# State-space parameters, tables and sines moved from the state-space stage into the first attention and feed-forward stages

## The chip, the cores and the metric

The kernel runs on one NeuronCore of a Trainium2 chip. The core has five engines with a queue of their own each: TensorE (PE, matrix multiplications, with PEld for its weight loads), VectorE (DVE), ScalarE (ACT), GpSimd (POOL) and SyncE (SP), which here only issues DMAs. They meet at semaphores. The metric is the device time of one launch in microseconds (us), the median of several runs. Everything is float32; the large products are computed from two-part splits (a high part and the remainder) in three matrix multiplications.

## What is computed

Two blocks of two layers each over a sequence of 512 tokens of 1024 channels. The kernel runs them as eight stages: two attention layers, then feed-forward, state-space (S5) mixer, feed-forward, feed-forward, convolution mixer, feed-forward. The part that the change touches is the S5 mixer:

```python
def s5_mixer(h, w_in, a_re, a_im, log_dt, b_re, b_im, c_re, c_im, d_skip, w_glu, b_glu, w_out):
    u = (h @ w_in).reshape(bsz, seq, 64, 16)
    dt = jnp.exp(log_dt)[:, None]
    mag = jnp.exp(dt * a_re)
    abar_re, abar_im = mag * jnp.cos(dt * a_im), mag * jnp.sin(dt * a_im)
    den = ar * ar + ai * ai
    nr = abar_re - 1.0
    f_re, f_im = (nr * ar + abar_im * ai) / den, (abar_im * ar - nr * ai) / den
    bb_re, bb_im = ...            # f * b, complex
    st = associative_scan(abar, bb @ u)           # over the 512 tokens
    y = Re(c @ st) + d_skip * u
    y = jax.nn.gelu(y)
    return (y * jax.nn.sigmoid(y @ w_glu + b_glu)) @ w_out
```

Nothing in `abar`, `f`, `bb` or in the powers and angles of `abar` depends on the tokens.

## The kernel before

The activation X stays in SBUF, channels on partitions, as 8 tiles of 128 x 512. Each stage has a function for each engine (`ffn_pe`, `ffn_act`, `s5_dve`, ...), and the order on an engine is the order in which these functions are written: nothing reorders it. Weights are streamed: SP loads a block of 128 x 2048 into one of two slots (`raw`), ACT copies its high part (`split_h`, L326), DVE takes the remainder (`split_l`, L331), and PE multiplies (`mm3`, L345 to L347, in `pe_block256`); a slot is used again when PE is through with it. In a feed-forward stage a pass of the loop (`pair`) is four tiles on PE: two of W1 and two of W3. ACT does two silus, a split, two copies of the hidden tile (L725) and a second split.

The S5 stage is cut into 8 chunks of tokens of length 8 within 64 positions (CL = 8, NC = 64) and worked off in 8 groups of channels, k = 0 to 7. Its course:

1. `in_pair` and two more blocks give u; `u_tile(o)` on DVE scales tile o, copies it in turned order into `rms`, and SP writes it to device memory with 8 DMAs. `u_tile(o)` waits with its copies until the DMAs of tile o-1 have landed.
2. DVE copies C (L1979), then computes the parameters on 128 x 64 tiles (L1982 to L2007 and L2028 to L2058), the phases of the powers 0 to 8 (L2014 to L2023, on 128 x 576), their products with the magnitudes (L2041 to L2046) and the scaled input matrices B1 and B2 (L2063 to L2073, on 128 x 1024). ACT gives exp and sines for it. `matrices(0)` (L2087 to L2090, six instructions) follows.
3. The loop over k. PE: `to_rows(k+1)` (8 transposes L1758, 8 products L1765), a swap of z (L1799), `toeplitz(k+1)` (L1775), `inputs(k+1)` (L1787), and the outputs of k (L1811, L1812). DVE: the turned inputs and the scan, which gives z(k) (L2113 to L2119), after the swap x(k) (L2127 to L2130), then `phases(k+2)` (L1910 to L1926, ten instructions) and `matrices(k+2)`. ACT: `rows(k+1)`, the sines `waves(k+2)`, the copy YS of the output (L1879), and `kernel_copy(k+1)` (L1863), for which `to_rows(k+2)` waits on PE since both use the same two banks. POOL: `decay(k)` (L2185) and `outmat(k)` (L2175 to L2178), which starts when the outputs of k-1 are through and for which the outputs of k wait. POOL also computes `phases(0)` and `phases(1)`.
4. SP carries YS through device memory to YR. After the loop DVE adds the skip (L2140), ACT applies gelu and takes the high part (L1885, L1888) for the 8 tiles one after another, DVE takes the remainders (L2144), and only behind all that do the splits of the next two weight blocks stand (L326, L331).

In the first attention stage `ahead` on ACT and `tiles` on DVE run in a loop while PE multiplies; in the feed-forward stages POOL has no work between `squares_pool` and the first squares of the output.

## Time and profile before

| what | us |
|---|---|
| median of 3 runs | 3165.71 (3160.33 to 3166.04) |
| the profiled execution's own time | 3160.42 |
| its span in the trace | 3158.6 |
| PE busy | 2817.4 (89%) |
| DVE busy | 1726.3 (55%) |
| ACT busy | 1149.2 (36%) |
| POOL busy | 354.2 (11%) |
| the S5 stage, 1297 to 1745 us: PE busy | 313.08 of 448 |
| the first feed-forward's loop, 943 to 1190 us: PE busy | 247.00 of 247 |

Times in the trace count from the span's start. The granted clock (PEclk) is given as a share of TensorE's full speed: 1.00 is 2.4 GHz, 0.50 is 1.2 GHz. A group has line, engine, operation, tiles, shapes, count, then busy us and mean ns, then idle us before it and what ended it. A timeline row has start, duration, engine, line, operation, the tiles written and read with their shapes, how many instructions are merged, and in brackets how long the engine stood idle before and what ended it. Busy PE time is modelled from pipelined multiplications; POOL's spans are rough.

### The profile page before, as it was taken

To read this page: it belongs to the slowest core of one execution; us is meant where nothing else is said; L and a number is where in the kernel's file an instruction comes from. 1 tells how busy PE (TensorE), PEld (TensorE's weight loads), DVE (VectorE), ACT (ScalarE), POOL (GpSimd) and SP (SyncE) were. 2 spreads that over 40 slices of the span, in tenths; PEclk is the share of its full clock that TensorE was granted. 3 is DMA by queue.
4 is the path that set the end of the run, shared out by engine and by line. 5 is a ranking of instruction groups with operands and counts; after the bars stand their busy time and mean duration, and the time that the engine had idled before them with its cause. 6 is when DMAs were issued, how large, how long until landed. Compare 5 with 4: busy or idle time off the path is not lost.

```text
span 3158.6 us, 37190 instructions
## 1 busy us (share of the span) xinstructions
PE 2817.4 (89%) x13972; PEld 2315.5 (73%) x13972; DVE 1726.3 (55%) x2526; ACT 1149.2 (36%) x1932; POOL 354.2 (11%) x307
## 2 busy tenths in 40 slices
PE   6987978979799999927768999999999998699998
PEld 5855767746588888827757888888888886588887
DVE  4378755388754442577744544254442588554423
ACT  3237833157733222302233322233222366432222
POOL 1011011020020000144311000020000112210000
PEclk9987989967999999966779999999999999899999
DMA  3220012310013323411122222322223211122232
GB/s 125 95 79 1 1 41 91 98 40 1 1 54 96 100 80 92 111 48 28 38 67 69 91 93 85 92 90 93 93 81 100 86 53 41 41 80 94 88 92 73
DMA packets 289664, 222.77 MB, mean 71 GB/s; under 512 B 43379, under 2 KB 285628, under 8 KB 289276
## 3 DMA queue, kind: packets, MB, share of 16 engines
q1 hardware_dynamic: 288604, 216.56, 22.8%
q0 software_dynamic: 928, 4.46, 0.4%
q8 instruction: 82, 1.34, 0.2%
q14 instruction: 50, 0.41, 0.0%
HBM read 214.70 MB, written 6.29 MB: 70 GB/s over the span
## 4 chain that ended last, share of the span: by engine, by line
PE 74%; DVE 10%; issue 5%; ACT 4%; DVEq 3%; POOLq 3%; POOL 2%; SPq 1%; DMA 0%; ACTq 0%
PE bank L345 22%; PE bank L347 21%; PE bank L346 21%; DVE WL L331 2%; PE bank L1316 1%; ACT WH L326 1%; PE bank L1303 1%; PE bank L1328 1%; DVE stats L1600 1%; POOLq L2179 1%; DVE XL L403 1%; DVE CV L984 1%; POOLq L2177 1%; PE bank L1330 1%; PE bank L1329 1%
## 5 line engine op out<-in xcount | busy, mean ns | idle before, releaser
L345 PE MATMUL bank<-XH,WH 128*128 128x512 f32 (+1 forms) x2688 | 999.2, 372 | 83.9 <-DVE WL L331 29.1
L347 PE MATMUL bank<-XH,WL 128*128 128x512 f32 (+1 forms) x2688 | 987.5, 367 | 0.0
L346 PE MATMUL bank<-XL,WH 128*128 128x512 f32 (+1 forms) x2688 | 983.2, 366 | 0.0
L331 DVE TENSOR_TENSOR WL<-raw,WH 128x2048 fp32r<-128x2048 f32 (+1 forms) x212 | 443.2, 2091 | 559.4 <-ACT WH L326 559.0
L345 PEld LDWEIGHTS bank<-XH,WH 128*128 128x128 f32 x2688 | 516.4, 192 | 178.2 <-DVE WL L331 40.4
L326 ACT ACTIVATE WH<-raw 128x2048 fp32r<-128x2048 f32 (+1 forms) x212 | 370.1, 1746 | 592.3 <-PE bank L347 592.3
L346 PEld LDWEIGHTS bank<-XL,WH 128*128 128x128 f32 x2688 | 516.8, 192 | 90.0 <-issue 1.0
L347 PEld LDWEIGHTS bank<-XH,WL 128*128 128x128 f32 x2688 | 515.6, 192 | 90.1
L345 PE MATMUL bank<-HH,WH 128*128 128x512 f32 (+1 forms) x792 | 294.0, 371 | 0.0
L347 PE MATMUL bank<-HH,WL 128*128 128x512 f32 (+1 forms) x792 | 293.7, 371 | 0.0
L346 PE MATMUL bank<-HL,WH 128*128 128x512 f32 (+1 forms) x792 | 291.7, 368 | 0.0
L725 ACT ACTIVATE HH<-work 128x512 f32 (+1 forms) x88 | 55.7, 633 | 369.6 <-DVE work L790 369.6
L834 POOL TENSOR_TENSOR ssq<-ssq,sq 128x512 f32<-128x512 f32 x24 | 30.9, 1290 | 1353.2 <-ACT sq L747 1353.2
L346 PEld LDWEIGHTS bank<-HL,WH 128*128 128x128 f32 x792 | 148.8, 188 | 29.1
L347 PEld LDWEIGHTS bank<-HH,WL 128*128 128x128 f32 x792 | 148.9, 188 | 28.4
L345 PEld LDWEIGHTS bank<-HH,WH 128*128 128x128 f32 x792 | 148.7, 188 | 27.1
L721 ACT ACTIVATE work<-work 128x512 f32<-128x512 f32 x88 | 55.2, 632 | 280.9 <-DVE work L783 280.8
L788 DVE TENSOR_TENSOR work<-bank,rstd 128x512 f32<-128x512 f32 x88 | 60.8, 691 | 175.9 <-PE bank L347 172.1
L783 DVE TENSOR_TENSOR work<-bank,rstd 128x512 f32<-128x512 f32 x88 | 60.2, 688 | 167.4 <-PE bank L347 158.0
L1451 ACT ACTIVATE E<-bank,stats 128x512 f32<-128x512 f32 (+1 forms) x176 | 113.0, 645 | 48.0 <-DVE stats L1602 31.0
L1600 DVE TENSOR_REDUCE stats<-bank 128x1 f32<-128x512 f32 (+1 forms) x176 | 107.8, 634 | 27.2 <-PE bank L1305 26.0
L414 POOL TENSOR_TENSOR ssq<-ssq,sq 128x256 f32<-128x256 f32 x112 | 96.3, 860 | 118.5 <-ACT sq L394 112.9
(364 smaller groups left out, 3599.4 us busy)
## 6 DMA issues: line engine op xcount, KB each, us to landing
raw<-in_ffn_w_dram SPq DMA_DIRECT2D x88, 1024.0 KB, 5.3
raw<-in_ffn_w_dram SPq DMA_DIRECT2D x64, 704.0 KB, 4.6
raw<-in_w_in_dram SPq DMA_DIRECT2D x24, 1024.0 KB, 5.2
raw<-in_w_out_dram SPq DMA_DIRECT2D x8, 1024.0 KB, 5.1
raw<-in_cv_w_in_dram SPq DMA_DIRECT2D x8, 1024.0 KB, 5.5
raw<-in_w_mem_kv_dram SPq DMA_DIRECT2D x4, 1024.0 KB, 5.3
raw<-in_s_w_in_dram SPq DMA_DIRECT2D x4, 1024.0 KB, 6.3
raw<-in_s_w_glu_dram SPq DMA_DIRECT2D x4, 1024.0 KB, 5.4
```

What stands on the lines that cost most here:

```text
L326: act.activation(WH[:, slot, 0:n * P], raw[:, slot, 0:n * P], ACT.Copy).then_inc(h_done, 1)
L331: dve.tensor_tensor(WL[:, slot, 0:n * P], raw[:, slot, 0:n * P], WH[:, slot, 0:n * P].bitcast(F32), ALU.subtract).then_inc(l_done, 1)
L345: pe.matmul(out, WH[:, slot, c:c + P], h, start=start, stop=False)
L346: pe.matmul(out, WH[:, slot, c:c + P], l, start=False, stop=False)
L347: return pe.matmul(out, WL[:, slot, c:c + P], h, start=False, stop=stop)
L414: ins = pool.tensor_tensor(ssq[:, HALF[h]], ssq[:, HALF[h]], sq[:, k % 2, HALF[h]], ALU.add)
L721: act.activation(work2[:, o, :], work1[:, o, :], ACT.Silu).then_inc(ss(s, "silu"), 1)
L725: act.activation(HH[:, bass.ds(2 * i + o, 1), :], work1[:, o, :], ACT.Copy).then_inc(ss(s, "hh"), 1)
L783: dve.tensor_tensor(work1[:, o, :], bank[o][:, :], rstd[:, :], ALU.mult).then_inc(acc_read, 1)
L788: dve.tensor_tensor(work1[:, o, :], bank[2 + o][:, :], rstd[:, :], ALU.mult).then_inc(acc_read, 1)
L1451: act.activation(E[:, m % 6, 0:nk * P], bank[m % 4][:, 0:nk * P], ACT.Exp, bias=stats[:, 1, m % 8:m % 8 + 1], scale=scale, accum_out=stats ...
L1600: dve.tensor_reduce(stats[:, 0, c:c + 1], bank[(m + i) % 4][:, 0:nk * P], AX, ALU.max)
```

## The change

- **First attention stage** (`attn0`). SP loads the S5 parameters behind its first four weight blocks (`par_sp`, five small DMAs). PE turns them after the memory blocks (`par_pe`, three small products). ACT takes exp, exp and two sines between the splits of the weight blocks; DVE computes the 128 x 64 part in three pieces behind three `tiles`. The loops of ACT and DVE there are written out. The results (FH, FL, MAG, FR, FI) stay in a new tile `par`.
- **First feed-forward stage** (`ffn0`). SP loads constants and B behind its first pair of blocks (`tab_sp`). POOL computes the table of powers and B1, B2 (`tab_pool`), sends them to device memory, and then wraps the phases for all 8 groups. ACT computes the sines (`tab_act`, `waves_act`) between the splits, at written places in its now unrolled loop, and issues their DMAs to device memory. The cosine is now taken as a sine of pi/2 less the absolute value, so that a group of phases needs 7 POOL instructions and not 10.
- **S5 stage.** Parameters, tables and phases are gone from DVE, ACT and POOL; SP loads the tables back, ACT issues the loads of the sines (`cs_load`). The skip, gelu and its splits are done inside the loop, for group k-2 and k-3 in pass k.
- MAG to the eighth power is read from `PW`.

```diff
         def ffn_sp(sp, s):
             pair(0)
+            if tab_stage(s):
+                tab_sp(sp, s)
             with sp.Fori(1, NP) as i:
...
+        def tab_sp(sp, s):
+            sp.wait_ge(mm_done, first_step[s])
+            sp.dma_start(s5cA[:, :], io["s5_c"]).then_inc(ss(s, "tab_c"), 16)
...
+            for dst, src in ((B1A[0:64], br), (B1A[64:128], bi), (B2A[0:64], bi), (B2A[64:128], br)):
+                sp.dma_start(dst, src).then_inc(ss(s, "b_in"), 16)
...
+        def wrap(pool, x, n, fh, fl, jj):
+            pool.tensor_tensor(x, fh, jj, ALU.mult)
+            pool.drain()
+            pool.tensor_scalar(n, x, ROUND, -ROUND, ALU.add, ALU.add)
+            pool.drain()
+            pool.tensor_tensor(x, x, n, ALU.subtract)
+            pool.drain()
+            pool.tensor_tensor(n, fl, jj, ALU.mult)
+            pool.drain()
+            pool.tensor_tensor(x, x, n, ALU.add)
+            pool.drain()
+            pool.tensor_scalar(n, x, ROUND, -ROUND, ALU.add, ALU.add)
...
+            pool.dma_start(tab_scr, tabA[:, :]).then_inc(ss(s, "tab_out"), 16)
+            for k in range(KD):
...
+                wrap(pool, PHA[:, :, :], PHN[:, :, :], fh, fl, jc)
+                if k >= 2:
+                    pool.wait_ge(ss(s, f"cs_out{k % 2}"), 16 * (k // 2))
+                pool.tensor_tensor(CSA[:, k % 2, 1], PHA[:, :, :], PHN[:, :, :], ALU.subtract).then_inc(ss(s, "ph"), 1)
...
+        def waves_act(act, s, k):
+            act.wait_ge(ss(s, "ph"), at(s, "ph", k + 1))
+            cos, sin = CSA[:, k % 2, 0], CSA[:, k % 2, 1]
+            act.activation(cos, sin, ACT.Abs).then_inc(ss(s, "abs"), 1)
+            act.wait_ge(ss(s, "abs"), at(s, "abs", k + 1))
+            act.activation(sin, sin, ACT.Sin, scale=s5cA[:, S5_SGN + 2:S5_SGN + 3])
+            act.activation(cos, cos, ACT.Sin, bias=eps_c[:, 1:2], scale=-TURN).then_inc(ss(s, "waves"), 1)
+            act.wait_ge(ss(s, "waves"), at(s, "waves", k + 1))
+            act.dma_start(cs_scr[k], CSA[:, k % 2]).then_inc(ss(s, f"cs_out{k % 2}"), 16)
...
         def ffn_act(act, s):
...
+            def pair(i, nxt, middle=()):
...
+                for k in middle:
+                    waves_act(act, s, k)
                 hidden(i, 0)
                 hidden(i, 1)
                 split_h(act, b0 + 2 * i + 3, 1, nxt, s0 + 4 * i + 4)
...
+            if tab_stage(s):
+                pair(1, 16)
+                tab_act(act, s)
+                pair(2, 16)
+                pair(3, 16)
+                waves_act(act, s, 0)
+                pair(4, 16, (1,))
+                waves_act(act, s, 2)
+                act.wait_ge(ss(s, "tab_out"), at(s, "tab_out", 16))
+                pair(5, 16, (3,))
+                waves_act(act, s, 4)
+                pair(6, 16, (5,))
+                waves_act(act, s, 6)
+                pair(7, 16, (7,))
+                for k in range(2):
+                    act.wait_ge(ss(s, f"cs_out{k}"), 16 * (KD // 2))
+                pair(8, 16)
+                pair(9, 16)
...
         def s5_sp(sp, s):
+            sp.wait_ge(ss(s, "tab_out"), 16)
+            sp.dma_start(tab[:, :], tab_scr).then_inc(ss(s, "tab_in"), 16)
...
         def s5_act(act, s):
+            def cs_load(k):
+                act.wait_ge(ss(s, "x"), at(s, "x", k - 1))
+                act.dma_start(CSW[:, k % 2], cs_scr[k]).then_inc(ss(s, f"cs_in{k % 2}"), 16)
...
                 if k + 1 < KD:
                     rows(k + 1)
-                if k + 2 < KD:
-                    waves(k + 2)
...
+                if k + 2 < KD:
+                    cs_load(k + 2)
                 if k + 1 < KD:
                     kernel_copy(k + 1)
+                if k >= 2:
+                    gelu(k - 2)
+            gelu(KD - 2)
+            gelu(KD - 1)
             split_h(act, b0 + 4, 0, 16, s0 + 6)
...
         def s5_dve(dve, s):
                 if k + 2 < KD:
-                    phases(dve, s, k + 2)
                     matrices(k + 2)
+                if k >= 2:
+                    skip(k - 2)
+                if k >= 3:
+                    low_y(k - 3)
```

Three places in the order of the engines show what moves. First ACT in the first feed-forward stage, pairs 4 and 5 of the changed kernel (L357 is the split of a weight block, L840 silu, L844 the hidden tile's copy, CSA the phases and sines):

```order
L357 ACTIVATE WH<-raw 128x2048
L777 ACTIVATE CSA<-CSA 128x520
L779 ACTIVATE CSA<-CSA,s5cA 128x520
L780 ACTIVATE CSA<-CSA,eps_c 128x520
L782 DMA cs_scr<-CSA 128x1040
L840 ACTIVATE work<-work 128x512 x2
L357 ACTIVATE WH<-raw 128x2048
L777 ACTIVATE CSA<-CSA 128x520
```

Before, that stretch was a loop of silus, a split, two copies and a split alone; no function table is loaded again between silu and the sines.

DVE behind the copies of C in the S5 stage of the kernel before (L1940 and L1947 are a `u_tile`, `sm` the parameters; between the first rows and the last stand 70 rows of parameters, of which these are the end):

```order
L1964 TENSOR_TENSOR sm<-SNJ,sm 128x64
L1964 TENSOR_TENSOR sm<-sm 128x64 x3
L1940 TENSOR_TENSOR UN<-bank,rstd 128x512
L1947 COPY rms<-UN 128x64 x8
L1959 TENSOR_SCALAR B<-B,s5c 128x1024
L2068 TENSOR_TENSOR Wt<-B,sm 128x1024
L1964 TENSOR_TENSOR W<-B,sm 128x1024
L2070 TENSOR_TENSOR B<-B,sm 128x1024
L1964 TENSOR_TENSOR B<-B,sm 128x1024
L2072 TENSOR_TENSOR B<-B,Wt 128x1024
L1964 TENSOR_TENSOR B<-B,W 128x1024
L2087 TENSOR_TENSOR Wt<-CSJ,B 128x512
```

The same place in the changed kernel (L2188 copies C, L2168 and L2175 are a `u_tile`, L2204 starts `matrices(0)`):

```order
L2188 TENSOR_SCALAR C<-bank,s5c 128x512 x2
L2188 TENSOR_SCALAR C<-bank 128x512 x2
L2168 TENSOR_TENSOR UN<-bank,rstd 128x512
L2175 COPY rms<-UN 128x64 x8
L2168 TENSOR_TENSOR UN<-bank,rstd 128x512
L2175 COPY rms<-UN 128x64 x8
L2204 TENSOR_TENSOR Wt<-tab 128x512
```

Between the copies of C and `matrices(0)` only two `u_tile`s are left.

ACT in a pass of the S5 loop of the changed kernel (L2094 and L2095 are `rows`, L2132 YS, L2115 the load of the sines, L2108 `kernel_copy`, L2119 gelu, L2122 the high part):

```order
L2100 ACTIVATE KS<-bank 128x128
L2132 ACTIVATE YS<-bank 128x512
L2115 DMA CSW<-cs_scr 128x1040
L2108 ACTIVATE MT<-bank 128x4x8x16 x2
L2119 ACTIVATE UN<-YR 128x512
L2122 ACTIVATE XH<-UN 128x512
L2094 ACTIVATE W<-bank 128x4x128
```

The two sines stood between L2100 and L2132; now a DMA issue stands between YS and `kernel_copy`, and gelu ahead of the next `rows`.

## Rows read from the trace of the kernel before

**Rows 1.** Windows: stretch, us, busy PE, PEld, DVE, ACT, POOL, clock, DMA share, GB/s.
```profile
943.00:1190.00 247.00, 247.00 (x1089) 199.97 (x1088) 109.64 (x112) 69.83 (x71) 0.00 (x0) 1.00 0.30 91
...
1434.18:1582.12 147.94, 116.46 (x714) 108.40 (x712) 115.53 (x152) 30.22 (x65) 56.37 (x43) 0.72 0.15 33
```
**Rows 2.** Timeline of DVE, from the copies of C to the first pass's inputs.
```profile
1338.34 1.14 DVE L1947 COPY rms<-UN 128x64 f32<-128x64 f32 x8 [4.57 <-DMA u_scr<-rms]
...
1357.96 0.69 DVE L1979 TENSOR_SCALAR C<-bank 128x512 f32<-128x512 f32 x1 [0.16 <-PE bank L1747]
...
1405.65 0.69 DVE L2087 TENSOR_TENSOR Wt<-CSJ,B 128x512 f32<-128x512 f32 x1
...
1434.18 0.69 DVE L2113 TENSOR_TENSOR work<-bank,COS 128x512 f32<-128x512 f32 x1 [4.88 <-PE bank L1787]
```
**Rows 3.** Timeline of PE: to_rows and inputs of group 0, inputs of a later group.
```profile
1414.13 1.97 PE L1758 MATMUL bank<-ident,Wt 128*128 128x128 f32 x8 [44.30 <-DVEq L2091]
1415.89 3.43 PE L1765 MATMUL bank<-C,Wt 128*128 128x16 f32 x16
...
1426.95 7.09 PE L1787 MATMUL bank<-U,W 128*128 128x64 f32 x32 [3.48 <-DVE UN L1940]
...
1486.94 3.68 PE L1787 MATMUL bank<-U,W 128*128 128x64 f32 x32
```
**Rows 4.** Timeline of DVE in the loop: phases, then matrices in two halves.
```profile
1443.04 0.70 DVE L1910 TENSOR_TENSOR PHA<-sm,s5c 128x520 f32<-128x520 f32 x1
...
1449.40 0.69 DVE L2087 TENSOR_TENSOR Wt<-CSJ,B 128x512 f32<-128x512 f32 x1
...
1451.54 0.69 DVE L2087 TENSOR_TENSOR Wt<-CSJ,B 128x512 f32<-128x512 f32 x1
```
**Rows 5.** Timeline of ACT in the loop and right behind it.
```profile
1451.67 0.60 ACT L1879 ACTIVATE YS<-bank 128x512 f32<-128x512 f32 x1 [1.07 <-PE bank L1812]
...
1473.21 1.08 ACT L1863 ACTIVATE MT<-bank 128x512 f32<-128x512 f32 x2
...
1585.53 0.60 ACT L1879 ACTIVATE YS<-bank 128x512 f32<-128x512 f32 x1 [11.71 <-PE bank L1812]
...
1601.85 0.60 ACT L1879 ACTIVATE YS<-bank 128x512 f32<-128x512 f32 x1 [14.75 <-PE bank L1812]
1602.46 1.28 ACT L1885 ACT_TABLE_LOAD   x1
...
1616.85 3.69 ACT L326 ACTIVATE WH<-raw 128x2048 fp32r<-128x2048 f32 x2
```
**Rows 6.** Timeline: the last skip on DVE, the next matmul on PE.
```profile
1610.10 1.15 DVE L2140 SCALAR_TENSOR_TENSOR YR<-UN,vecT,YR 128x512 f32<-128x512 f32 x1 [10.29 <-DMA YR<-y_scr]
...
1621.12 0.79 PE L345 MATMUL bank<-XH,WH 128*128 128x512 f32 x1 [19.31 <-DVE WL L331]
```
**Rows 7.** Timeline of PE (one of the parameters' products) and of SP's queue (one issue).
```profile
1332.25 0.43 PE L1739 MATMUL bank<-KS,ones 1*128 1x64 f32 x2
...
959.08 0.37 SPq L337 DMA_DIRECT2D raw<-in_ffn_w_dram  x1
```
**Rows 8.** Timeline of POOL: a group of phases, the first and last of its instructions.
```profile
1367.43 1.58 POOL L1910 TENSOR_TENSOR PHA<-sm,s5c 128x520 f32<-128x520 f32 x1
...
1383.50 1.28 POOL L1926 TENSOR_TENSOR COS<-COS,PHA 128x520 f32<-128x520 f32 x1
```
**Rows 9.** Groups by line and form; those of DVE from 943 to 1190.
```profile
L943 POOL TENSOR_TENSOR ssq<-ssq,sq 128x512 f32<-128x512 f32 x12 | 25.6, 2131 | 538.4 <-ACT sq L879 538.1
...
L331 DVE TENSOR_TENSOR WL<-raw,WH 128x2048 fp32r<-128x2048 f32 x20 | 45.9, 2293 | 35.6 <-ACT WH L326 35.6
L790 DVE TENSOR_TENSOR work<-work 128x512 f32<-128x512 f32 x22 | 15.2, 692 | 2.0
```
**Rows 10.** Timeline of DVE: one pair of ffn0; one product of matrices(0) beside POOL.
```profile
1021.78 2.29 DVE L331 TENSOR_TENSOR WL<-raw,WH 128x2048 fp32r<-128x2048 f32 x1 [0.99 <-ACT WH L326]
...
1028.82 0.69 DVE L783 TENSOR_TENSOR work<-bank,rstd 128x512 f32<-128x512 f32 x1 [4.15 <-PE bank L347]
...
1409.44 1.59 DVE L2087 TENSOR_TENSOR Wt<-CSJ,B 128x512 f32<-128x512 f32 x1
```

More of the change, by code:

```diff
@@ L33 @@
 ROUND = 1.5 * 2 ** 23
+HALF_PI = math.pi / 2
 NMEM = 256
@@ L1188, in program, with ts, tt @@
         LAG_V = 6
+        FH, FL, MAG, FR, FI, PW = (par[:, n, :] for n in range(6))
+        AR, AI, DT, M, TH, MC, EM, T0 = (smr[:, n, :] for n in range(8))
+        T1, RED, EX, S2, NR, DEN, SN = (smt[:, n, :] for n in range(7))
+        def ts(eng, out, in0, a, b, op0, op1=None):
+            if op1 is None:
+                eng.tensor_scalar(out, in0, a, None, op0)
+            else:
+                eng.tensor_scalar(out, in0, a, b, op0, op1)
+            eng.drain()
+        def tt(eng, out, a, b, op):
+            eng.tensor_tensor(out, a, b, op)
+            eng.drain()
@@ new lines, in stt, with par_sp, par_pe @@
+        def stt(eng, out, a, c, b, op0, op1):
+            eng.scalar_tensor_tensor(out, a, c, b, op0, op1)
+            eng.drain()
+        def par_sp(sp, s):
+            for i, n in enumerate(("s5_a_re_2", "s5_a_im_2")):
+                for h in range(2):
+                    sp.dma_start(a_rows[0:GROUPS, i, 64 * h:64 * h + 64], io[n][0]).then_inc(ss(s, "par_in"), 16)
+            sp.dma_start(dt_row[:, :], io["s5_log_dt_2"]).then_inc(ss(s, "par_in"), 16)
+        def par_pe(pe, s):
+            pe.wait_ge(ss(s, "par_in"), at(s, "par_in", 16 * 5))
+            for i in range(2):
+                pe.transpose(bank[5][:, 64 * i:64 * i + 64], a_rows[0:GROUPS, i, :], ident[0:GROUPS, 0:GROUPS])
+            pe.matmul(bank[5][:, 128:192], ones[0:1, :], dt_row[:, :], start=True, stop=True)\
+              .then_inc(ss(s, "par_t"), 1)
@@ L1392, in head_rms @@
                    .then_inc(ss(s, "grms"), 1)
-            with act.Fori(1, 4) as i:
-                for q in range(2):
-                    ahead(i, q)
+            if s == stages[0]:
+                ahead(1, 0)
+                par_exp_act(act, s)
+                ahead(1, 1)
+                ahead(2, 0)
+                par_mag_act(act, s)
+                par_sin_act(act, s)
+                ahead(2, 1)
+                ahead(3, 0)
+                ahead(3, 1)
+            else:
+                with act.Fori(1, 4) as i:
+                    for q in range(2):
+                        ahead(i, q)
             ahead(4, 0)
@@ L1550, in head_norm @@
                    .then_inc(ss(s, "gn"), 1)
-            with dve.Fori(2, 4) as i:
-                for q in range(2):
-                    tiles(i, q)
+            if s == stages[0]:
+                tiles(2, 0)
+                par_angle_dve(dve, s)
+                tiles(2, 1)
+                par_mag_dve(dve, s)
+                tiles(3, 0)
+                par_input_dve(dve, s)
+                tiles(3, 1)
+            else:
+                with dve.Fori(2, 4) as i:
+                    for q in range(2):
+                        tiles(i, q)
             tiles(4, 0)
@@ L1734, in s5_pe @@
             in_pair(pe, s, b0, j0)
-            pe.wait_ge(ss(s, "par_in"), at(s, "par_in", 16 * 6))
-            for i in range(2):
-                pe.transpose(bank[5][:, 64 * i:64 * i + 64], a_rows[0:GROUPS, i, :], ident[0:GROUPS, 0:GROUPS])
-            pe.matmul(bank[5][:, 128:192], ones[0:1, :], dt_row, start=True, stop=True)\
-              .then_inc(ss(s, "par_t"), 1)
             pe.wait_ge(ss(s, "c_in"), at(s, "c_in", 16 * 4))
@@ L2038, in s5_dve @@
-            tt(v(NR), v(EM), CSJ[:, 1, :], ALU.mult)
-            stt(v(NR), v(T0), -2.0, v(NR), ALU.mult, ALU.add)
-            two(dve.tensor_copy(v(PW), v(MAG)))
-            for j in range(1, J):
-                dve.tensor_tensor(CSJ[:, j, :], CSJ[:, j, :], v(PW), ALU.mult)
-                dve.tensor_tensor(SNJ[:, j, :], SNJ[:, j, :], v(PW), ALU.mult)
-                dve.drain()
-                if j < CL:
-                    tt(v(PW), v(PW), v(MAG), ALU.mult)
-            tt(v(DEN), v(AR), v(AR), ALU.mult)
```

364 lines of the change are left out of this document (185 added, 179 removed).

## The prediction

> **What bounds the kernel now.** I read the windows first, by stage [rows 1]. In the first feed-forward's loop PE is busy all 247.00 us, at clock 1.00: there a microsecond taken from PE's feed is lost and one given to another engine costs nothing, as long as ACT and DVE (69.83 and 109.64 busy) keep their splits on time. POOL is at 0.00. In the S5 loop, 1434.18 to 1582.12 and seven passes long, PE is busy 116.46 of 147.94 us, DVE 115.53, POOL 56.37, at clock 0.72: no engine is full, so a chain across engines sets the pace. The timelines of DVE and PE then show three places that the change can shorten. First the start: the last copy of C begins at 1357.96, `matrices(0)` only at 1405.65 and the first pass's inputs at 1434.18 [rows 2]; PE stands still for 44.30 us for it [rows 3]. Then the loop, where DVE puts `phases` between its scan and `matrices` [rows 4]. Then the tail, in which ACT does eight gelus ahead of the next split [rows 5] and PE restarts 19.27 us behind YS(7), at 1621.12 [rows 6].
>
> **The start of S5.** Behind 1357.96 + 0.69 = 1358.65 DVE has 47.0 us of parameters, powers and B before `matrices(0)`, with `u_tile(4)` and `u_tile(5)` in between [rows 2]. In the new order only these two `u_tile`s stand there. A `u_tile` is a scaling and copies of 1.14, say 2.4 with its waits, to 1361.1; the next one's copies wait for the DMAs of this one, 4.57 us of waiting in the row [rows 2], some 5.5 with the scaling and the landing's start: 1366.9; with copies to 1368.2. `matrices(0)` is two halves of 1451.54 - 1449.40 = 2.14 each [rows 4], 4.3: 1372.5. It has to find the table loaded, a DMA issued right at the stage's start some 70 us earlier: hidden. `to_rows(0)` is 1.97 and 3.43, overlapping, 5.2 from 1414.13 [rows 3]. In the trace of before 1434.18 - 1414.13 = 20.05 us pass from there to the first pass on DVE. Two pieces of that shrink. `matrices(1)` no longer meets POOL at full length; beside POOL a product of it took 1.59 [rows 10] against 0.69 alone [rows 4]. And `inputs(0)` took 7.09 at the low clock of an engine just woken against 3.68 later [rows 3]; PE still wakes here, yet from a shorter sleep, so I take the middle, 5.4. That makes about 16.2: the first pass starts at 1372.6 + 16.2 = 1388.8. **Gain 45.4**; with inputs at 7.09 and nothing gained beside POOL 41.5, with 3.68 47.1.
>
> **The loop.** From YS(0) at 1451.67 to YS(6) at 1585.53 six periods take 133.86 us, 22.3 each [rows 5]. The chain of a period: DVE's scan, `phases` of 1449.40 - 1443.04 = 6.36 [rows 4], `matrices` of 4.3 (more beside POOL), then `to_rows` on PE. Without `phases` DVE's work per pass is 3.4 + 2.0 (scan and x) + 4.3 + 1.15 for `skip` [rows 6] + about 0.6 for `low_y`, 11.5 and beside POOL some 15; POOL's is 56.37 / 7 = 8.1 busy [rows 1]. PE's is 116.46 / 7 = 16.6 [rows 1], 17.1 with the gaps within a pass. What is late next is PE itself and what stands between its passes: outputs of k, YS (0.60), now the issue of `cs_load` (a DMA issue that wasn't there; on SP's queue one takes 0.37 [rows 7]), `kernel_copy` (1.08) [rows 5], for which `to_rows` waits, and about 0.1 of semaphores: 2.2. So the period becomes 17.1 + 2.2 = 19.3, three shorter. ACT's gelu and high part ((1616.85 - 1603.74) / 8 = 1.64 [rows 5]) stands behind `kernel_copy`, beside PE's `to_rows`, where the next `rows` isn't wanted for 5 us; the issue of the sines' load has a whole pass to land. **Gain 6 x 3.0 = 18.0.** Its ends: 0 (below, the third rival) and 41 (the second).
>
> **The tail.** YR(7) came back through device memory at 1610.10, 8.25 us behind YS(7) [rows 5, 6]. That trip stays. Then `skip` 1.15 [rows 6], gelu and high part 1.64, one split on ACT (half of 3.69), the remainder on DVE 2.29 [rows 10] and 0.3 between: 8.25 + 1.15 + 1.64 + 1.85 + 2.29 + 0.3 = 15.5 against 19.27. **Gain 3.8.** The load of gelu's table (1.28, [rows 5]) moves into the loop, where ACT idles 11.71 before YS [rows 5]; it is hidden there, but one load for silu's or sigmoid's side stays as before.
>
> **What the other stages pay.** In the first attention stage PE gets three small products; the last row of them is 0.43 [rows 7], all three with their wait **0.8**. SP's five issues and DVE's small operations stand ahead of work that isn't waited for for some 7 us of each 11-us block, so I set them at nothing; if the splits were late by all of them it would be 3.
>
> In the first feed-forward stage POOL is the new runner. One group of phases, ten instructions, took 1383.50 + 1.28 - 1367.43 = 17.35 us [rows 8]; seven remain, without three of them: about seven tenths, 12.0. Beside DVE's long splits it will be slower: POOL's product of 512 took 2.13 beside work on ACT and DVE [rows 9] against 1.28 for one of 520 [rows 8]. DVE's splits fill 45.9 of 247 us [rows 9], so I take 12.0 / (1 - 0.186) = 14.7, and since only part of the seven meets a split, 14.0. POOL starts at 944; the powers 12.6, B 18.8, products 10.3 and waits bring it to 991.5; group 7 is ready at 991.5 + 8 x 14.0 = 1103.5. ACT comes to its place for group 7 at 1099.2, and would stand 4.3 us. A wave itself costs ACT an absolute value and two sines, each near the 0.60 of a copy of 512 [rows 5], an issue of 0.37 [rows 7] and three waits on itself, 2.5. Behind the wave stand the hidden tile's copies and the second split, and DVE's remainder of that split, done at 1024.07 in the pair shown, is wanted by PE near 1028.8 [rows 10]: 4.8 slack. PE thus loses 4.3 + 2.5 - 4.8 = **2.0**. Bounds: 0 (12.0 per group) and 34 (first rival). The sine's table: the compiled order has no load between silu and sine, so the 1.28 of a load [rows 5] isn't paid. The Trainium skill (ScalarE: Activation LUTs, What ACT_TABLE_LOAD costs) puts a switch at about 2.66 us with its drain; no row here shows the drain, since YS and the load lie back to back (1601.85 + 0.60, 1602.46), and by the page the order without loads would still pay nothing.
>
> **The sum.** -45.4 - 18.0 - 3.8 + 0.8 + 2.0 = -64.4, on the profiled execution's 3160.42: 3096.0. The median of the runs is 5.3 higher, 3165.71: 3101. Anything within 0.2%, some 6 us, could not be told from no change.
>
> **The rivals.** *POOL is shut out by DVE* (chance 0.16). If a product with two SBUF inputs on DVE and one on POOL never run together, POOL stands while the splits (45.9 us), the hidden products (15.2) [rows 9] and the remainders of the hidden tiles (as many again) run, 76 of 247 us, 31%, and a group takes 12.0 / 0.69 = 17.4. The head, stretched alike, ends at 996.5; group 7 is ready at 1135.7, 36.5 late, and PE loses 36.5 + 2.5 - 4.8 = 34. Time 3101 + 32 = 3133. For it speaks 1.59 against 0.69 [rows 10]; against it that such a row can just as well be a queue of a part of an instruction. The Trainium skill (SBUF — State Buffer, SBUF: two separate sides) says that the pair of ports is an exclusive lock for the whole instruction; by it this rival would be the forecast, by the rows POOL's 2.13 [rows 9] stays short of 1.28 + 2.29.
>
> *PE stays awake* (0.17). The loop's clock is 0.72 [rows 1] because PE stands several us in each pass; with gaps of 2 us instead, the granted clock may stay high, and PE's 16.6 us at 0.72 are 12.0 at 1.00; with the gaps within a pass and clock that isn't all regained 13.2, the period 15.4, six times 3.9 less: 3078. Against it: PE still stands twice in each pass, and behind a stop of 3.48 us `inputs` ran at 7.09 [rows 3].
>
> *The loop isn't shortened* (0.12). If `matrices` beside POOL (which starts with the outputs) still ends as late, or POOL's `outmat`, some 9, and the outputs behind it close the cycle, the 22.3 stay and the gain of 18 goes: 3119.
>
> *Slower* (0.03). POOL's pace decides it: the gains of 67 less 0.8 are eaten when group 7 is 69 late, at (1099.2 + 69 - 991.5) / 8 = 22 us a group. Per group that is seven instructions of 3.1, against 2.13 for a product beside others [rows 9]; it needs a DVE that holds POOL for far longer than it is busy, 109.64 of 247 us [rows 1]. At 23 us a group: 3175. *It doesn't do what it says* (0.02), the sines being waited for again at the start of S5 (their DMAs, half a megabyte each, landing late): 3160.
>
> **How the numbers follow.** Forecast 0.50, between 3086 and 3114, plus the five above. Likeliest: 3101. The range leaves out the slower case, the fast half of the clock's case and the slow half of POOL's: 3074 to 3132. Faster by over 0.2%: all but the last two, 0.95; within 0.02; slower 0.03.
>
> **What would show it.** PE's wait ahead of `to_rows(0)` near 0 to 5 us instead of 44.30; YS to YS 19.3; PE's restart 15.5 behind YS(7); seven POOL instructions in 14.0 us and ACT waiting for POOL only at the last one or two waves; PE's loop in the first feed-forward stage longer by 2, the first attention by 1. If POOL needs over 15 us a group, the first feed-forward takes back from the gain at eight for one; if the clock in the S5 loop is over 0.9, the second rival holds; if DVE still waits for the sines, the last one.

## The result, and the profile after

| | us |
|---|---|
| before, median | 3163.86 (3160.33 to 3166.04) |
| changed, median | 3087.26 (3084.13 to 3089.03) |
| changed / before | 0.9765 (0.9753 to 0.9777) |
| changed, the profiled execution | 3087.88 (span 3086.1) |
| forecast | 3101 (3074 to 3132) |

The kernel became 76.6 us faster by the medians, 72.5 us by the two profiled executions. The forecast was 64.4. Where the profiled difference lies is read from marks that both traces have (all in us):

| stretch | before | after | difference | forecast |
|---|---|---|---|---|
| span's start to the last copy of C | 1357.96 | 1357.94 | 0.0 | +2.8 |
| last copy of C to the first pass on DVE | 76.22 | 32.53 | -43.7 | -45.4 |
| first pass on DVE to YS(0) | 17.49 | 16.89 | -0.6 | - |
| YS(0) to YS(6), six periods | 133.86 | 109.09 | -24.8 | -18.0 |
| YS(6) to YS(7) | 16.32 | 16.07 | -0.3 | - |
| YS(7) to PE's restart | 19.27 | 15.49 | -3.8 | -3.8 |

They add up to -73.1; behind PE's restart the changed kernel is 0.6 us longer. Two of these marks move from run to run. In the twelve runs below all is the same up to the last copy of C, except that e5 loads POOL; in the other eleven that copy starts between 1355.89 and 1360.50. In the six of them that leave the start of the S5 stage alone, and in the changed kernel, the stretch to the first pass on DVE takes 31.0 to 33.8. So the 0.0 of the first row is 0 within some 2 us, and differences of 1 or 2 us in the second row mean nothing.

The windows of the changed kernel that answer to [rows 1] and to the loop (stretch, its us, busy us of PE, PEld, DVE, ACT, POOL, clock, DMA share, GB/s). The second runs from YS(0) to YS(6), the third and fourth are about two single passes:

```profile
943.00:1190.00 247.00, 247.00 (x1087) 199.87 (x1086) 123.33 (x112) 86.80 (x98) 134.07 (x94) 1.00 0.36 115
1407.36:1516.45 109.09, 98.55 (x636) 91.66 (x636) 60.76 (x87) 28.40 (x57) 48.73 (x42) 0.78 0.28 74
1407.70:1425.30 17.60, 15.88 (x106) 14.74 (x106) 9.09 (x14) 3.45 (x9) 7.44 (x8) 0.81 0.28 76
1425.30:1444.60 19.30, 17.52 (x106) 16.38 (x106) 10.21 (x16) 3.52 (x9) 7.58 (x8) 0.73 0.25 69
```

The same stretch from YS(0) to YS(6) in the kernel before, and PE's wait for `matrices` at the head of its first pass:

```profile
1451.67:1585.53 133.86, 102.37 (x636) 95.35 (x636) 105.72 (x135) 27.05 (x59) 55.77 (x42) 0.73 0.17 36
```

```profile
1455.34 1.97 PE L1758 MATMUL bank<-ident,Wt 128*128 128x128 f32 x8 [3.71 <-DVEq L2091]
```

In the first feed-forward PE is as full as before, 247.00 of 247, although POOL now works 134.07 us there. The loop isn't longer either: from the first split of DVE to one at its end 246.64 us pass before (944.66 to 1191.30) and 246.65 after (944.14 to 1190.79). Nothing was paid. In the S5 loop DVE fell from 105.72 us in 133.86 to 60.76 in 109.09, and PE is now busy nine tenths of it, at clock 0.78 where it was 0.73.

The timeline of DVE at the start of the S5 stage, which answers to [rows 2] (L2188 the last copy of C, L2175 the copies of `u_tile(4)` and `(5)`, L2204 `matrices(0)`, L2240 the first pass):

```profile
1357.94 0.69 DVE L2188 TENSOR_SCALAR C<-bank 128x512 f32<-128x512 f32 x1 [0.16 <-PE bank L2008]
1358.55 0.68 DVE L2168 TENSOR_TENSOR UN<-bank,rstd 128x512 f32<-128x512 f32 x1
1359.32 4.55 DVE L2175 COPY rms<-UN 128x64 f32<-128x64 f32 x8
...
1368.99 1.11 DVE L2175 COPY rms<-UN 128x64 f32<-128x64 f32 x8 [4.52 <-DMA u_scr<-rms]
1370.02 0.68 DVE L2204 TENSOR_TENSOR Wt<-tab 128x512 f32<-128x512 f32 x1
...
1390.47 0.69 DVE L2240 TENSOR_TENSOR work<-bank,CSW 128x512 f32<-128x512 f32 x1 [4.76 <-PE bank L2048]
```

`matrices(0)` starts 12.1 us behind the last copy of C, where it was 47.7. The eight copies at 1359.32 took 4.55 instead of 1.11: `outmat(0)` on POOL starts at the same time, since it too now waits for nothing but C.

ACT at the end of a pass and PE behind it (answering to [rows 5] and to the wait ahead of `to_rows`), then the tail ([rows 5, 6]):

```profile
1407.36 0.60 ACT L2132 ACTIVATE YS<-bank 128x512 f32<-128x512 f32 x1 [11.78 <-PE bank L2073]
1407.37 0.33 ACTq L2115 DMA_DIRECT2D CSW<-cs_scr  x1
1407.86 1.08 ACT L2108 ACTIVATE MT<-bank 128x512 f32<-128x512 f32 x2
...
1409.08 1.11 PE L2019 MATMUL bank<-ident,Wt 128*128 128x128 f32 x8 [1.76 <-ACT MT L2108]
...
1532.52 0.60 ACT L2132 ACTIVATE YS<-bank 128x512 f32<-128x512 f32 x1 [12.87 <-PE bank L2073]
...
1548.01 0.79 PE L376 MATMUL bank<-XH,WH 128*128 128x512 f32 x1 [15.53 <-DVE WL L362]
```

Before, PE waited for `matrices` in each of the six passes, 3.71 to 6.81 us. Now it waits for `kernel_copy` (MT), 1.76 us, in every pass.

### The profile page after: what moved, and what is told of

Read it like the earlier page. It is cut to its first block, busy times and chain, and to the rows that moved or that the text cites. A ratio compares the mean times of both kernels' runs of the same rounds, so it can differ in the third digit from the quotient of the medians.

```text
span 3086.1 us, 37069 instructions
## 1 busy us (share of the span) xinstructions
PE 2804.6 (91%) x13972; PEld 2303.3 (75%) x13972; DVE 1653.5 (54%) x2427; ACT 1156.4 (37%) x1943; POOL 448.2 (15%) x383
## 4 chain that ended last, share of the span: by engine, by line
PE 75%; DVE 10%; issue 5%; ACT 3%; DVEq 3%; POOLq 2%; POOL 1%; SPq 1%; DMA 0%; ACTq 0%
PE bank L376 22%; PE bank L378 22%; PE bank L377 22%; DVE WL L362 2%; PE bank L1566 1%; ACT WH L357 1%; DVE stats L1870 1%; PE bank L1553 1%; PE bank L1578 1%; DVE XL L434 1%; DVE CV L1126 1%; DVEq L1871 1%; POOLq L2303 1%; POOLq L2301 1%; DVE E L1897 1%
## 5 line engine op out<-in xcount | busy, mean ns | idle before, releaser
L357 ACT ACTIVATE WH<-raw 128x2048 fp32r<-128x2048 f32 (+1 forms) x212 | 370.0, 1746 | 581.5 <-PE bank L378 581.5
L844 ACT ACTIVATE HH<-work 128x512 f32 (+1 forms) x88 | 55.7, 632 | 362.3 <-DVE work L930 362.3
L840 ACT ACTIVATE work<-work 128x512 f32<-128x512 f32 x88 | 55.2, 632 | 270.5 <-DVE work L923 270.5
L1566 PE MATMUL bank<-ident,E 128*128 128x128 f32 x448 | 82.8, 308 | 34.3 <-DVE PTL L1879 31.1
```

The lines of the kernel that those rows point to most:

```text
L357: act.activation(WH[:, slot, 0:n * P], raw[:, slot, 0:n * P], ACT.Copy).then_inc(h_done, 1)
L840: act.activation(work2[:, o, :], work1[:, o, :], ACT.Silu).then_inc(ss(s, "silu"), 1)
L844: act.activation(HH[:, bass.ds(2 * i + o, 1), :], work1[:, o, :], ACT.Copy).then_inc(ss(s, "hh"), 1)
L1566: mm = pe.transpose(bank[4 + u % 2][:, c * P:(c + 1) * P], E[:, SCORE0[u] % 6, c * P:(c + 1) * P], ident[:, :])
```

## Experiments

All times are medians; a ratio is to the kernel before, with its 95% interval. The changed kernel itself stands at 0.9765, so 0.001 is 3.2 us. The runs came in three groups on chips where the kernel before took 3160.24 (e1 to e4), 3158.26 (e5 to e8) and 3161.57 (e9 to e12). "V(0)" is the first pass on DVE, counted from the last copy of C.

### Is the gelu free inside the loop?

```diff
                 if k + 1 < KD:
                     kernel_copy(k + 1)
-                if k >= 2:
-                    gelu(k - 2)
-            gelu(KD - 2)
-            gelu(KD - 1)
+            for k in range(KD):
+                gelu(k)
...
                     matrices(k + 2)
-                if k >= 2:
-                    skip(k - 2)
-                if k >= 3:
-                    low_y(k - 3)
...
+            for k in range(KD):
+                skip(k)
+            for k in range(KD):
+                low_y(k)
```

> The changed kernel with skip, gelu, high part and remainder put back behind the S5 loop; all else stays. The prediction's view: they lie off the chain of the loop, so YS to YS stays at 18.2 us and only the tail changes: PE restarts 19.3 us behind YS(7) instead of 15.5. Time 3087.3 + 3.8 = 3091. Rival: in the loop they cost, since the table load and gelu put the next rows of W back by about 1 us in every pass and skip and remainder add 1.8 us to DVE; then the loop gets shorter by some 0.5 us a pass, 3 in all, and the time is 3088 or less.

Measured: 3089.93, ratio 0.9781 (0.9765 to 0.9797). The mean period is 18.18, as with the gelu in the loop, and PE restarts 19.26 us behind YS(7) instead of 15.49. That is the tail's 3.8 us to a tenth, and the rival's shorter loop isn't there: 1.8 us of skip and remainder per pass on DVE cost the loop nothing. By time alone the two kernels can't be told apart (their intervals overlap); the marks in the trace carry this one.

### What set the old pace of the loop?

```diff
                 if k + 2 < KD:
+                    dve.tensor_tensor(a, fh, jc, ALU.mult)
+                    dve.drain()
+                    dve.tensor_scalar(n, a, ROUND, -ROUND, ALU.add, ALU.add)
+                    dve.drain()
...
                     matrices(k + 2)
```

> The changed kernel with ten instructions of 128 x 520 (the phases' own sequence, into a scratch tile that nothing reads) put back on DVE between x(k) and matrices(k+2) in six passes. The prediction's view: the 6.4 us of phases ahead of matrices set the old pace, because to_rows waits for matrices and these run into POOL's outmat; YS to YS goes from 18.2 back to 21.5 to 22.5, the time to 3087.3 + 6 x 4.1 = 3112. Rival: the pace came from something else that left with them (sines on ACT, their wait); then the period stays below 19.5 and the time below 3096.

Measured: 3124.24, ratio 0.9880 (0.9863 to 0.9896). The periods are 23.69 to 26.24, 24.35 on average. Ten instructions on DVE, at 0.43 to 0.70 us each, cost six times 6.2 us. The timeline of one pass shows how: the remaining halves of `matrices` fall together with POOL's `outmat`, and PE waits 6.72 us for them.

```profile
1434.63 1.44 DVE L2209 TENSOR_TENSOR Wt<-Wt,Wx 128x512 f32<-128x512 f32 x1
1436.14 1.44 DVE L2206 TENSOR_TENSOR Wt<-tab 128x512 f32<-128x512 f32 x1
1437.49 1.75 DVE L2207 TENSOR_TENSOR Wx<-tab 128x512 f32<-128x512 f32 x1
1439.31 1.43 DVE L2209 TENSOR_TENSOR Wt<-Wt,Wx 128x512 f32<-128x512 f32 x1
```

In the changed kernel each of these takes 0.68 or 0.69: there `matrices` starts when `outmat` is through. The expected 21.5 to 22.5 were too low, since the loop is even slower than the old one (22.3). The skip and the remainder, 1.1 and 0.7 us that the old loop didn't hold, may be the difference; no run isolates it.

The same ten instructions behind `matrices(k + 2)`:

```diff
                 if k + 2 < KD:
+                    matrices(k + 2)
                     dve.tensor_tensor(a, fh, jc, ALU.mult)
...
-                    matrices(k + 2)
```

> As the run before, but the same ten instructions stand behind matrices(k+2) instead of ahead of them: the same work on DVE in another place. If the place decides (PE waits for matrices, which POOL's outmat stretches), the period stays near 18.2 to 19.5, time 3087 to 3095. If the amount decides (DVE is full), it is as slow as the run before, near 3112.

Measured: 3120.36, ratio 0.9875 (0.9859 to 0.9892), mean period 23.84. The expectation that the place decides fell, at least for these two places. But DVE isn't full either: it is busy 118.39 of the 143.02 us from YS(0) to YS(6). Now `matrices` are in time, and what comes late is the scan: PE's swap of z waits 4.07 to 6.61 us for it, and the last of the ten instructions themselves run beside `outmat`, 1.17 to 1.45 us each instead of 0.43 to 0.70.

```profile
1407.65 1.45 DVE L2282 TENSOR_TENSOR DA<-DA,DN 128x520 f32<-128x520 f32 x1
...
1416.30 2.08 PE L2062 MATMUL bank<-work,s5c 128*128 128x512 f32 x2 [4.24 <-DVE work L2248]
```

So the loop is a ring, from the scan over PE's swap, x(k) and `matrices` back to the scan of k + 1, and 5.9 us put into it on DVE lengthen it by about as much in either of the two places. That isn't so for every amount: the 1.8 us of e1 cost nothing, and how much fits in free was not measured. The prediction named only the arc by way of `matrices`.

### What does PE's gap of 1.76 us cost?

MT in two buffers, so that `kernel_copy(k + 1)` can run ahead of YS(k):

```diff
-        MT = sb("MT", [P, GS, CL, GCH], F32, rb2)
+        MT = sb("MT", [P, 2, GS, CL, GCH], F32, rb2)
...
-                if k >= 1:
-                    act.wait_ge(ss(s, "ydone"), at(s, "ydone", k))
+                if k >= 2:
+                    act.wait_ge(ss(s, "ydone"), at(s, "ydone", k - 1))
...
                     rows(k + 1)
+                    kernel_copy(k + 1)
                 act.wait_ge(ss(s, "ydone"), at(s, "ydone", k + 1))
```

> The changed kernel with MT in two buffers; kernel_copy(k+1) stands ahead of YS(k) on ACT. In the trace of the changed kernel PE waits 1.76 us for MT in each pass, with clock 0.78 in the loop. If only that gap counts: period 18.2 - 1.8 = 16.4, seven gaps, time 3087.3 - 12.5 = 3075. If the gap is also what keeps the clock low (the rival of the prediction in which PE stays awake), the clock in the loop goes to over 0.9, PE's 16.4 us per pass shrink towards 13, a wait for DVE or the sines' load ends last next, period 14 to 15.5, time 3055 to 3068.

Measured: 3085.50, ratio 0.9757 (0.9741 to 0.9773): not to be told from the changed kernel. PE never waits for MT now, but other waits of 1.3 to 2.1 us came in four of the six passes: for U, for the scan and for ACT's `rows`. The periods are 16.2 to 21.3 us, and that their mean is again 18.18 is chance. In the longest pass PE waited for U:

```profile
1462.05 1.12 PE L2060 MATMUL bank<-work,s5c 128*128 128x512 f32 x2 [1.26 <-DVE work L2245]
...
1466.65 5.98 PE L2048 MATMUL bank<-U,W 128*128 128x64 f32 x32 [1.69 <-DMA U<-u_scr]
```

and what followed ran at the low clock: 5.98 us for products that take 3.68 at the high one. The clock over the loop is 0.76, no higher than with the gap. Neither expectation held.

With the load of U(k + 2) ahead of the eight DMAs of YS(k):

```diff
             for k in range(KD):
                 sp.wait_ge(ss(s, "ys"), at(s, "ys", k + 1))
+                if k + 2 < KD:
+                    sp.wait_ge(ss(s, "u_in"), at(s, "u_in", 16 * (k + 2)))
+                    u_load(k + 2)
                 for t in range(CL):
...
-                if k + 2 < KD:
-                    sp.wait_ge(ss(s, "u_in"), at(s, "u_in", 16 * (k + 2)))
-                    u_load(k + 2)
```

> MT in two buffers as in e4_mt_double, and SP issues the load of U(k+2) ahead of the eight DMAs of YS(k) instead of behind them. In e4's trace PE waited 1.69 us for U in one pass, and that pass took 21.25 us instead of 16.3. If the load of U is what took the gain back, all periods come near 16.3 and the time is 3087.3 - 7 x 1.9 = 3074. Rival: with PE at MT's heels the waits move to DVE (scan and x beside POOL's outmat); then periods of 19 to 21 us remain and the time is 3080 to 3086.

Measured: 3081.17, ratio 0.9756 (0.9739 to 0.9772), by time the same as e4. In the trace the mean period is 17.12, single ones from 12.41 to 21.55. The wait for U is gone; waits for the scan of 2.48 and 4.89 us stand in its place, the rival's, beside others of 1.27 and, for `rows`, 1.93. Three windows of this run show how the clock goes with the waits: a whole pass without one, 22 us behind the wait of 1.93, and a pass with the wait of 1.27:

```profile
1404.37:1416.78 12.41, 12.41 (x108) 11.93 (x107) 8.19 (x11) 3.60 (x9) 8.73 (x7) 1.00 0.39 108
...
1442.00:1464.00 22.00, 22.00 (x99) 20.97 (x99) 11.14 (x14) 5.10 (x10) 9.47 (x9) 0.50 0.21 61
...
1473.25:1487.10 13.85, 12.58 (x107) 11.90 (x106) 11.96 (x13) 5.01 (x11) 9.60 (x7) 1.00 0.34 97
```

PE stayed at the high level without any filler in the first, stayed at the low one for 22 us without a stop in the second, and wasn't slowed by its wait in the third. So taking the stop for MT away doesn't bring the clock back by itself.

The gap filled instead of removed:

```diff
                 mm.then_inc(ss(s, "ydone"), 1)
+                if k + 2 < KD:
+                    for _ in range(3):
+                        pe.matmul(bank[7][:, :], ident[:, :], tab[:, 0:T], start=True, stop=True)
```

> The changed kernel with three products of 128 x 512 into a bank that nothing reads, between the outputs of a group and to_rows of the next (six passes), where PE waits 1.76 us. Nothing else moves. Three of them take 1.7 us at clock 1 and 3.1 at the low one. By the prediction's rival (PE stays awake) the gap is what keeps the clock at 0.78: without it the clock in the loop goes over 0.9 and the period from 18.2 to 13.5 to 16, time 3074 to 3083. By the prediction the clock stays where it is, the period becomes 18.2 + up to 1.3, time 3087 to 3095.

Measured: 3073.41, ratio 0.9721 (0.9705 to 0.9737): 14 us faster than the changed kernel by three useless products per pass (an f32 product leaves two rows in the trace, so they are six there). The periods are 15.03 to 15.81 (mean 15.37 against 18.18), and the clock in the loop is 1.00:

```profile
1409.91:1502.13 92.22, 91.08 (x672) 78.42 (x671) 73.10 (x87) 28.60 (x58) 52.71 (x42) 1.00 0.32 87
```

and in the timeline of PE, one pass:

```profile
1424.74 2.79 PE L2078 MATMUL bank<-tab,ident 128*128 128x512 f32 x6
1427.37 1.04 PE L2019 MATMUL bank<-ident,Wt 128*128 128x128 f32 x8
1428.24 1.86 PE L2026 MATMUL bank<-C,Wt 128*128 128x16 f32 x16
1429.95 1.10 PE L2060 MATMUL bank<-work,s5c 128*128 128x512 f32 x2
```

The 8 products of L2026 (16 rows) take 1.86 us here and 3.43 in the changed kernel. The filler takes 2.63 us of each pass (the expectation had 1.7), 0.9 more than the gap. So the gap's price was not 1.76 us a pass but 1.76 and what the low clock took behind it, 2.8 + 0.9 = 3.7 us; filling it gains 2.8 us a pass net. The filler does two things at once, it closes the stop and it adds products of 128 x 512, and no run tells which of them holds the clock. That PE may still wait a little is in this trace: 0.23 to 0.51 us in three passes, at 1.00.

### What does POOL cost in the first feed-forward?

```diff
             for k in range(KD):
...
+                pool.tensor_tensor(PHN[:, :, :], fh, jc, ALU.mult)
+                pool.drain()
                 wrap(pool, PHA[:, :, :], PHN[:, :, :], fh, fl, jc)
+                pool.tensor_scalar(PHA[:, :, :], PHA[:, :, :], 0.0, 0.0, ALU.add, ALU.add)
+                pool.drain()
+                pool.tensor_scalar(PHN[:, :, :], PHN[:, :, :], 0.0, 0.0, ALU.add, ALU.add)
+                pool.drain()
```

> The changed kernel with three more instructions (a product and two two-step additions of 0 on 128 x 520, which change no value) in each of POOL's eight groups of phases in the first feed-forward stage, so ten as before the change. In the trace of the changed kernel a group takes 12.9 us and group 7 is ready at 1099.1, when ACT comes to it, at no cost for PE. With three more (1.1, 1.95, 1.95 and their steps) a group takes about 18.6 and group 7 is ready at 1146, 47 late. By the prediction's slack (4.8 us behind the wave, 2.5 of it used up) PE loses 45, time 3132. By the trace of the changed kernel ACT also stands 1.55 and 4.97 us for the hidden tiles behind that wave, so the slack is about 11 and PE loses 36: 3123. If POOL is held by DVE for the whole of each split (the prediction's first rival), a group takes over 22 and the time passes 3150.

Measured: 3126.59, ratio 0.9892 (0.9874 to 0.9910). A group takes (1149.41 - 1017.50) / 7 = 18.84 us and the last is ready at 1150.7, 51.6 later than in the changed kernel; the last copy of C comes at 1400.22 instead of 1357.94, 42.3 later. The mark of C moves by some 2 us between runs, but by this pair 9.3 us of lateness are free, between the 4.8 of the prediction (which left out that ACT has to wait for the hidden tiles in any case) and the 11 of the trace. ACT waits for POOL at each of the last six waves, 12.1 to 13.3 us:

```profile
1149.41 1.31 POOL L769 TENSOR_TENSOR CSA<-PHA,PHN 128x520 f32<-128x520 f32 x1
1150.75 0.64 ACT L783 ACTIVATE CSA<-CSA 128x520 f32<-128x520 f32 x1 [13.32 <-POOL CSA L769]
```

The strong form of the rival, POOL held for the whole of each split (over 22 us a group, over 3150), fell. Seven instructions per group instead of ten are not a detail of the change: with ten, some 40 of its 73 to 77 us are gone.

### The start: POOL beside DVE, and the order on DVE

```diff
             pool.wait_ge(ss(s, "c_cp"), at(s, "c_cp", 4))
+            pool.wait_ge(ss(s, "s"), at(s, "s", 1))
             outmat(0)
```

> The changed kernel with outmat(0) on POOL held back until inputs(0) are through. In the trace of the changed kernel the copies of u_tile(4) take 4.55 us beside outmat(0), 1.1 alone, and matrices(0) wait for them by way of u_tile(5). If that meeting costs the start what it shows, the first pass on DVE starts 3.3 us earlier (32.5 to 29.2 us behind the last copy of C), time 3084. Rival: outmat(0) then runs into DVE's x(0) and matrices(2) and the outputs of group 0 come as late as now; time 3087 unchanged.

Measured: 3081.78, ratio 0.9754 (0.9738 to 0.9771). The copies of `u_tile(4)` take 1.12 instead of 4.55, V(0) comes at 28.56 instead of 32.53, and most of the 4 us stays: YS(0) is 3.3 us earlier by the same mark. Both lie outside the spread of the runs with the old start (31.0 to 33.8 for V(0)); by time alone the gain can't be told from nothing.

```profile
1359.98 1.12 DVE L2175 COPY rms<-UN 128x64 f32<-128x64 f32 x8
```

With `matrices(0)` ahead of `u_tile(5)` and `matrices(1)` behind `u_tile(7)`:

```diff
             u_tile(4)
-            u_tile(5)
             dve.wait_ge(ss(s, "tab_in"), at(s, "tab_in", 32))
...
             matrices(0)
+            u_tile(5)
             u_tile(6)
-            matrices(1)
             u_tile(7)
+            matrices(1)
```

> The changed kernel with matrices(0) on DVE ahead of u_tile(5) and matrices(1) behind u_tile(7). In the trace of the changed kernel PE waits 4.73 us for matrices(0), which wait for u_tile(5)'s copies and so for a DMA. If that order is what sets the first pass, to_rows(0) starts at once behind the last block and the first pass 5 to 6 us earlier: 27 us behind the last copy of C instead of 32.5, time 3082. Rival: the chain of u_tile and its DMAs sets the end anyway, by the scaling of tile 7; then the first pass moves by less than 2 us.

Measured: 3085.15, ratio 0.9767 (0.9751 to 0.9783). V(0) at 30.68, 1.85 earlier and hardly outside that spread: the rival was right. PE starts `to_rows(0)` without a wait, but three of the six products of `matrices(0)` took 1.6 us beside `outmat(0)`, and `matrices(1)` then stood behind the DMA of `u_tile(7)`.

Both, with only the scaling of tile 7 (`u_scale`, split off from `u_tile`) ahead of `matrices(1)` and its copies behind:

```diff
             matrices(0)
+            u_tile(5)
             u_tile(6)
+            u_scale(7)
             matrices(1)
-            u_tile(7)
+            u_tile(7, scale=False)
```

> Only the start of the S5 stage against the changed kernel: outmat(0) held back as in e6_outmat_late, matrices(0) ahead of u_tile(5), the scaling of tile 7 ahead of matrices(1) and its copies behind. e6 brought the first pass on DVE from 32.5 to 28.6 us behind the last copy of C; e7_matrices_first, beside outmat(0), to 30.7. If the two meet (POOL beside DVE, and the order of matrices), together they bring it to 24 to 25 us, time 8 below the changed kernel's, 3079. Rival: they share one gain, and it stays at 28: 3083.

Measured: 3080.84, ratio 0.9749 (0.9733 to 0.9765). V(0) at 22.08 us, 10.4 earlier than in the changed kernel and more than expected; the span is 8.1 us shorter. This and the two before are small steps, seen in the marks, at the edge of what the times tell.

### Together

The start of e9 with MT in two buffers and U first:

> e9_start and e8_mt_double_u_first together. e8's trace had periods from 12.4 to 21.6 us, 17.1 on average, with waits for the scan where DVE works beside POOL's outmat. The two parts don't touch each other's time: the sum of both, about 8 + 5 us below the changed kernel, 3074; if the irregular periods come out worse from another start, 3080.

Measured: 3065.38, ratio 0.9700 (0.9683 to 0.9716). V(0) at 25.46, mean period 15.73 (12.40 to 19.11). Some 21 us faster than the changed kernel, more than the sum of both parts. The fast passes are as rare as in e8; the slow ones are shorter, the longest 19.11 instead of 21.55, and the clock in the loop is 0.89 instead of 0.82. Why, no run shows. The start kept only 7 of e9's 10.4 us: `outmat(0)`, held until the inputs are through, now meets the copies of `u_tile(7)`, which take 4.03 us instead of 1.10.

```profile
1377.39 4.03 DVE L2178 COPY rms<-UN 128x64 f32<-128x64 f32 x8 [0.25 <-DMA u_scr<-rms]
```

This beats both kernels.

With the skip and the remainder moved to where DVE waits for PE's swap:

```diff
+                if k >= 3:
+                    skip(k - 3)
+                if k >= 4:
+                    low_y(k - 4)
                 dve.wait_ge(ss(s, "zswap"), at(s, "zswap", k + 1))
...
                     matrices(k + 2)
-                if k >= 2:
-                    skip(k - 2)
-                if k >= 3:
-                    low_y(k - 3)
```

> e11_combined, with skip and remainder (for group k-3 and k-4) on DVE between the scan and x(k), where it waits for PE's swap, and gelu for group k-3 on ACT. In e8 the scan of a group came up to 4.9 us late for PE with skip and remainder (1.1 and 0.7, up to 2.7 beside POOL) ahead of it. If they stood in its way, periods fall by 1 to 2 us each: 3062 to 3070. If DVE's meeting with POOL is what makes it late, nothing moves: within 3 us of e11_combined.

Measured: 3065.00, ratio 0.9694 (0.9678 to 0.9711), mean period 15.39, but the tail 16.96 instead of 15.35: no difference from e11. The periods alternate, 12.4 and 17.8, 13.0 and 17.8: in the slow passes PE waits 1.8 to 2.5 us for the scan. In the second of them the scan stood beside `outmat` and took 2.13 us, where it takes 1.23 alone. e9's start with e10's filler, which by their marks might be faster than either, wasn't run.

## Why the prediction was right, point by point

**The start.** Forecast 45.4, measured 43.7, a miss no larger than the spread of this mark. The chain came out as written, `u_tile(5)`, its DMA, `matrices(0)`, `to_rows(0)`, but the copies of `u_tile(4)` took 3.4 us longer than the 1.14 of [rows 2], because `outmat(0)` had moved up with everything else. (The other terms before `to_rows(0)` were taken 1.6 us too long, so only 1.8 of the 3.4 show; from `to_rows(0)` to the first pass it is 16.2 as forecast.) The step "a `u_tile` is a scaling and copies of 1.14" priced the moved instructions in the surroundings they had before. e6 shows the cost and gets it back, at least in the marks.

**The loop.** Forecast 3.0 us a period, measured 4.1; this term holds most of the error. Mechanism and next bound were right: PE waits for `kernel_copy` alone. Two sizes were off. Between the passes stand 1.76 us and not 2.2, since the DMA issue of `cs_load` runs on ACT's queue beside YS (1407.37 beside 1407.36), and `kernel_copy` starts 0.50 behind YS's start. And PE's part of a pass was taken as 17.1, as in the old loop at clock 0.72, where it is 15.9 at clock 0.81 in four of six passes and 17.5 at 0.73 in two. That the old 22.3 came from `phases` ahead of `matrices` is borne out in part: back in that place they bring the wait for `matrices` back (e2), but behind `matrices` they cost nearly the same by the wait for the scan (e3). The amount in the ring counts, not that place.

**The tail.** Forecast 15.5 us behind YS(7), measured 15.49; e1 undoes it alone and gets 19.26.

**The other stages.** The first attention stage was priced at 0.8, and a split of DVE there does come 0.7 us later behind the three products (109.23, where the split before it stood at 102.88; in the kernel before 109.05 and 103.37). Whether it stays lost can't be read: from the split at 103 us to the first one of the feed-forward stage 841.29 us pass before, 841.26 after, and 839.0 to 842.5 in the runs above, which are the same there. In the first feed-forward the price was 2.0 and measured 0.0 (246.64 and 246.65 us). A group takes 12.9 us and not 14.0, and the slack is 9 and not 4.8.

**The rivals.** "POOL is shut out by DVE" failed in its sum and not in its mechanism. In the trace of the changed kernel, POOL and DVE in the first feed-forward:

```profile
1021.20 2.92 DVE L362 TENSOR_TENSOR WL<-raw,WH 128x2048 fp32r<-128x2048 f32 x1 [0.89 <-ACT WH L357]
...
1020.65 1.32 POOL L763 TENSOR_TENSOR CSA<-PHA,PHN 128x520 f32<-128x520 f32 x1
1022.13 2.91 POOL L711 TENSOR_TENSOR PHA<-par,s5cA 128x520 f32<-128x520 f32 x1 [0.16 <-issue]
```

The split began while POOL's product ran, and took 2.92 instead of 2.29; POOL's next product began while the split ran, and took 2.91 instead of 1.06, until the split was through. In both cases the later one is longer by about the time that the earlier one still had to run. The Trainium skill (SBUF — State Buffer, SBUF: two separate sides) has the pair of ports as an exclusive lock for the whole instruction, taken by whoever starts first; these rows, products on both sides, agree. Another pair doesn't: a split that began 0.10 us into a two-step addition on POOL ran beside it for 1.86 us and took 2.66, only 0.37 longer.

```profile
998.69 1.96 POOL L713 TENSOR_SCALAR PHN<-PHA 128x520 f32<-128x520 f32 x1 [4.72 <-issue]
...
998.79 2.66 DVE L362 TENSOR_TENSOR WL<-raw,WH 128x2048 fp32r<-128x2048 f32 x1 [1.00 <-ACT WH L357]
```

Over POOL's 56 instructions only 13.6 us are lost, 1.7 a group, where the rival's time share of 31% made 5.4. POOL loses much, 1.85 us, only where its instruction starts while a split is running, four times here; where it started first, the split bears the loss. And the rival's base of 12.0 us already held such losses, since the undisturbed durations of the seven come to 9.9 and with their steps to about 11.

"PE stays awake" was called for a loop whose gaps shrink to 2 us. The clock rose only from 0.73 to 0.78, so the case didn't come; but e10 shows that its mechanism is real once the gap is filled. That the period there is 15.4, the rival's figure (by which it gave 3078), is luck: it had 13.2 for PE and 2.2 between the passes, e10 has about 12.4 for PE, 2.63 of filler and little else. What was wrong is the condition: with 1.76 us in each pass the clock still falls. "The loop isn't shortened" didn't come. For "slower", e5 puts a point on the line: at 18.84 us a group, 42 us are lost. Continued at one us lost for each us late, the whole gain of 73 would be gone at about 23 us a group, near the 22 of the prediction; no run went there.

## What to carry to other kernels

Price a moved instruction by its new neighbours: here the freed POOL work ran beside DVE's copies at once and took back 4 of some 48 us. In a loop that is a ring over several engines, an engine's idle time is not slack: 5.9 us of work a pass on a DVE that was busy 10 of 18 cost 6.2 and 5.7 us, while 1.8 us cost nothing. And read the clock beside the gap: PE's short wait in each pass cost more by the clock behind it than by itself, and filling it was worth almost four times what the tail gained.
